# Two activation buffers of a two-block transformer kernel at other SBUF addresses

## What is computed

```python
gu = h @ w_gate_up            # 1024 x 5632
g, u = jnp.split(gu, 2, axis=-1)
return (jax.nn.silu(g) * u) @ w_down   # 2816 x 1024
```

## The kernel before

| Buffer | used by TensorE as | before | with the change |
|---|---|---|---|
| `whi`, `wlo` | weights, or moving in v2 and mdn | 0 | 0 |
| `xa` | moving; weights in v2 | 64 | 32 |
| `xb` | moving | 64 | 64 |
| `ghid` | moving | 64 | 0 |
| `hid` | weights | 0 | 0 |

## Time and profile before

### The profile page before, as it was taken

The page is one execution under the profiler, slowest core; times in us unless marked ns, Lnnn a source line. Parts: engine busy times, 40 slices in busy tenths (PEclk is TensorE's granted clock), DMA queues, the critical chain, the costliest instruction groups (busy, mean ns, idle before and its releaser), DMA issues.

```text
span 977.0 us, 19940 instructions
## 1 busy us (share of the span) xinstructions
PE 970.0 (99%) x7076; PEld 902.9 (92%) x7076; DVE 696.9 (71%) x1046; ACT 589.4 (60%) x1050; POOL 268.0 (27%) x241
## 2 busy tenths in 40 slices
PE   9999999999999999999999999999999999999998
PEld 7999899999998899999999888888889989998887
DVE  7987766665668778666565799987877877664443
ACT  7556755554557767545554678968585577664332
POOL 2431233220102223223210136542031546441000
PEclk9999999999999999999999999999999999999999
DMA  9785565655543245555455554654444536556531
GB/s 335 256 316 187 188 212 174 213 167 190 206 173 129 88 138 207 198 189 204 164 203 205 176 177 165 216 181 164 173 147 170 201 130 218 205 179 207 181 130 43
DMA packets 37712, 180.92 MB, mean 185 GB/s; under 512 B 3472, under 2 KB 7824, under 8 KB 19984
## 3 DMA queue, kind: packets, MB, share of 16 engines
q1 hardware_dynamic: 37504, 179.99, 52.5%
q10 hardware_dynamic: 144, 0.08, 0.1%
HBM read 179.01 MB, written 1.05 MB: 184 GB/s over the span
## 4 chain that ended last, share of the span: by engine, by line
PE 95%; DVE 2%; ACT 1%; issue 1%; POOL 1%; DMA 1%; SPq 0%; POOLq 0%; DVEq 0%
PE bank L502 26%; PE bank L496 19%; PE bank L498 17%; PE bank L500 17%; PE bank L540 4%; PE bank L539 4%; PE bank L538 4%; DVE wlo L1534 1%; DVE xa L1588 1%; PE bank L751 1%; PE bank L626 1%; DMA x<-in_x 1%; PE bank L735 1%; PE bank L765 0%; PE bank L976 0%
## 5 line engine op out<-in xcount | busy, mean ns | idle before, releaser
L1534 DVE TENSOR_TENSOR wlo<-raw,whi 128x1024 fp32r<-128x1024 f32 (+1 forms) x289 | 354.2, 1226 | 148.0 <-ACT whi L1009 147.1
L1009 ACT ACTIVATE whi<-raw 128x1024 fp32r<-128x1024 f32 (+2 forms) x289 | 302.1, 1046 | 202.2 <-PE bank L502 196.7
L502 PE MATMUL bank<-xa,wlo 128*128 128x256 f32 x1536 | 308.7, 277 | 0.0
L502 PEld LDWEIGHTS bank<-xa,wlo 128*128 128x128 f32 x1536 | 254.9, 188 | 22.9
L498 PE MATMUL bank<-xa,whi 128*128 128x256 f32 x904 | 227.3, 276 | 0.0
L500 PE MATMUL bank<-xa,whi 128*128 128x256 f32 x904 | 227.2, 276 | 0.0
L496 PE MATMUL bank<-xa,whi 128*128 128x512 f32 x632 | 203.3, 397 | 0.7 <-POOL wlo L2242 0.5
L498 PEld LDWEIGHTS bank<-xa,whi 128*128 128x128 f32 x904 | 169.7, 188 | 0.0
L500 PEld LDWEIGHTS bank<-xa,whi 128*128 128x128 f32 x904 | 169.7, 188 | 0.0
L2130 POOL TENSOR_TENSOR gate<-act,rbc 128x256 f32<-128x256 f32 x44 | 69.0, 1569 | 158.2 <-ACT act L1174 153.0
L496 PEld LDWEIGHTS bank<-xa,whi 128*128 128x128 f32 x632 | 99.6, 188 | 7.6 <-issue 1.7
(11 more groups left out here) (233 smaller groups left out, 1530.0 us busy)
## 6 DMA issues: line engine op xcount, KB each, us to landing
raw<-in_stream SPq DMA_DIRECT2D x137, 1024.0 KB, 4.8
raw<-in_stream SPq DMA_DIRECT2D x42, 512.0 KB, 4.8
raw<-in_stream SPq DMA_DIRECT2D x8, 768.0 KB, 4.1
bias<-in_bias SPq DMA_DIRECT2D x1, 3072.0 KB, 11.4
raw<-in_stream SPq DMA_DIRECT2D x8, 256.0 KB, 5.5
x<-in_x SPq DMA_DIRECT2D x4, 256.0 KB, 5.4
out<-x SPq DMA_DIRECT2D x3, 256.0 KB, 2.2
cons<-in_cons SPq DMA_DIRECT2D x1, 576.0 KB, 9.1
```

The source lines that it names most:

```text
L502: ins = pe.matmul(narrow, wlo[:, slot, at + i, :], X[:, k, 0, :], start=False, stop=last and i == len(tiles) - 1)
L1009: act.activation(whi[:, p, 0:kts, :].rearrange("p k m -> p (k m)"), src, ACT.Copy)\
L1534: dve.tensor_tensor(wlo[:, p, 0:kts, :].rearrange("p k m -> p (k m)"), src, whi[:, p, 0:kts, :].rearrange("p k m -> p (k m)").bitcast(F32) ...
```

## The change

The filler ahead of `xa` shrinks from 16 to 8 words of 4 bytes, and one of 8 words is put between `xa` and `xb`, so that `xb` and all behind it stay where they were. The filler ahead of `ghid` goes. No instruction, wait or transfer is added, taken away or moved: on all five engines the order of the instructions is the same.

```diff
         x = sb("x", [P, KT, TOK])
-        sb("before_xa", [P, 16])
+        sb("before_xa", [P, 8])
         xa = sb("xa", [P, KT, 2, TOK], F32R)
+        sb("before_xb", [P, 8])
         xb = sb("xb", [P, KT, 2, TOK], F32R)
...
         regiond = ExitStack()
-        regiond.enter_context(nc.sbuf_tensor("before_ghid", [P, 16], F32))
         ghid = regiond.enter_context(nc.sbuf_tensor("ghid", [P, FT, 2, TOK], F32R))
```

## The result

| | before | with the change |
|---|---|---|
| median, same chip | 985.19 us (981.31 to 987.43, 4 runs) | 1000.1 us (999.8 to 1000.33, 4 runs) |
| profiled execution, its own time | 978.75 us | 1000.33 us |
| its span | 977.0 us | 998.3 us |

The ratio of the medians is 1.0154, with a 95% interval of 1.0124 to 1.0184: slower by 1.5%, outside the range that was given. The two profiled executions differ by more, 21.3 us of span.

What follows compares the result with a forecast made beforehand. TensorE's matmul count times its start-to-start step was taken as the bound. Wide `xa` -3.3 and `xa` as weights -0.6, others 0, made -3.9 us, from 985.37 to 981.5 us; range 978.0 to 997.5.

Steps and rivals of the forecast that it cites:

- The clean step is a floor: Narrow matmuls of `xa` at 0.1133 us cannot step faster, so the change can only leave that step or break it.
- The forecast is wrong if the narrow step moves at all: Sign against the forecast: any change of the 0.1133 us narrow step; the wide one keeping its 5.52 us was the other.
- xa narrow: 2712 matmuls of 256 columns at L498, L500 and L502: taken as 0, bounds 0 to 11.3 or 18.1 us slower.
- a second influence: `xb` narrow, also 64 behind, stepped at 0.1175 us, 0.0042 more than `xa`; read as a clean and a slow rhythm.
- the lower of the two prices offered from above: Upper bound for narrow `xa` falling into the slow rhythm of `xb`: 2712 x 0.0042 = 11.3 us; the other was 18.1.
- The same step for ghid: 1056 narrow matmuls going to difference 0: taken as 0, from above 4.4 or 7.0 us slower.
- xa wide: 664 matmuls at L496 and L626 losing 0.005 us each: all taken as gone, -3.3 us; bounds -3.3 to +1.1.
- a matter of rhythm and half a step nearer to the clean case may suffice: Reason given for taking all 3.3 us of the wide `xa` loss as gone, and the 0.6 us as weights.
- xa as weights: 96 matmuls at L538 to L540 losing 0.0067 us each: taken as -0.6 us, bounds 0 and -0.6.
- `xb` and all behind it keep their places: nothing of their own: Term for the unmoved buffers, `xb`, `hid` and the attention's `bias`: no cost or gain counted.
- rivals 3 and 4: Narrow `xa` loses its clean rhythm, 11.3 us, chance 0.15; `ghid` alone does, 4.4 to 7.0 us, 0.10; both together 0.04.
- rival 5: Timed runs 6.6 us above the profile hold slow narrow matmuls, which the new placement avoids: 978.8 us, chance 0.06.

Runs made afterwards that it cites:

- the map: Kernels computing nothing of the reference, TensorE alone streaming at many operand distances; the second goes from wide to narrow pieces in 16-byte steps. Narrow loss 0.0 to 6.7 ns per step.
- the profile of 985.65 us: The unchanged kernel before, profiled again on the same chip: 985.65 us, with up0 clean and up1 and dn1 slow; a further execution took 979.78 us.
- the first map: TensorE alone, computing nothing of the reference, five streams per placement in 32-byte steps, a short matmul ahead of each; narrow loss 0.0 to 6.7 ns per step.

## Why the prediction was wrong

**What held.** The bound was read rightly: TensorE's pace is the time, no wait moved, and the whole difference lies in start-to-start steps. The clean step is a floor, as argued: no stretch of any run went under 0.1133. That addresses matter, and by the relation of the two operands, held too (everything 64 bytes later changed nothing). "The forecast is wrong if the narrow step moves at all" named the sign that came. The forecast was 981.5 us and the range ended at 997.5; measured were 1000.1.

**The step that failed, xa narrow.** "I take 0, because moving minus weights address is 64 in the clean rows 5 and 6 and 0 in the clean rows 7, and 32 lies between." Both halves fell. The dependence can't be interpolated: the map goes 0.0 at 112, 5.3 at 128, 0.0 at 192 and 5.9 at 208. And 64 is not a clean place but one with two rhythms; the earlier trace rows happened to show the clean one. The earlier trace rows had shown the slow one at the same distance, and I set it aside as a second influence instead of reading it as the price at hand. Measured 11.0 us, where the lower of the two prices offered from above was 11.3. That the two agree is in part luck: the price was that of `xb` at 64, and place 32 charges 4.45 ns in up0 and up1 but 3.33 elsewhere.

**The same step for ghid.** The 0 rested on the earlier trace rows, where each load of weights goes with 512 columns and the weights are the activation. With 256 columns, difference 0 costs 6.65 ns a step in every stream: 7.0 us, the upper bound. The prediction had the doubt ("though with twice the columns per weight load") and gave it 0.10.

**xa wide, the wrong sign.** Forecast -3.3, measured +2.6. The loss before was 4.5 us and not 3.3, since the one stretch of the earlier trace rows lies in a mild stage. The map has 3.3 or 6.6 ns per step at 32 and 2.5 at 64, so the sign is the place's, and the kernel's mean of 5.3 per step (7.0 us / 1328) lies between the map's two values. At 64 the kernel's mean is 3.4 against the map's 2.5, and what adds to it was not found. That the loss was "a matter of rhythm and half a step nearer to the clean case may suffice" was again interpolation.

**xa as weights.** Forecast -0.6, measured 0.0: 32 costs there what 64 does.

**Not in the sum.** `xb` narrow, unmoved, lost 1.9 us more: in o and bl it took the slow rhythm (0.00 to 4.44 ns a step), in which wo stood before. "`xb` and all behind it keep their places: nothing of their own" counted addresses and not what stands ahead of a stream.

**The rivals.** The profiled pair, +21.3 us, is rivals 3 and 4 together (11.3 + 7.0 = 18.3) with the wide and `xb` terms on top. Against the median only 15 us show, and rival 5's mechanism says why, with its sign turned: a gap of this size was slow narrow streams in the profile of 985.65 us, 6.2 of it up1 and dn1. I wrote that nothing in the trace ties the gap to this, and gave 0.06; that second profile ties it, while the timed runs themselves were not traced. By it the median execution of the kernel before had paid some 6 us already, so the change could only take 15 more. With the change all four runs lie within 0.53 us, although place 32 has two prices as well.

## What to carry to other kernels

Where TensorE is the bound, read its step from start to start, stretch by stretch, and compare like matmuls with each other; the busy share says 99% in both cases here. The distance between the starts of the moving operand and of the weights is worth mapping with TensorE alone, entered as the kernel enters it, before a buffer is moved: 192 bytes (of 256) behind the weights gave 978.4 to 979.7 us in 12 runs, 64 gave 978.5 to 990. A map shows which prices a place can charge and not which one the kernel will pay: 192 was slow in four of five streams of the first map and clean in nearly all of the kernel, and 32 paid more in the kernel than in any narrow stream of the maps. And when the runs of a kernel scatter in groups while one profile looks clean, profile it again: that profile may be the lucky execution, and a price read from one execution is then not the price of the kernel.

## What had not been expected of the hardware

- With a load of weights for each 256 columns in float32r, the step depends on the distance of two start addresses with a period of 256 bytes, not monotonically: 113.3 ns clean, 120.0 at distance 0, with neighbours 16 bytes apart that differ by up to 6.6 ns (96 and 112).
- One placement can have two steady rhythms (narrow, 0.0 or 4.4 ns at 64, 3.3 or 4.45 at 32), each kept over stages of 192 to 864 matmuls, and different in two executions of the same kernel. At 64 the slow one was kept from up0 to dn0 and from up1 to dn1. In the kernel before, the four groups that fit this span 9 us.
- Place 192 has the slow rhythm too, but `ghid` at 192 ran clean right behind slow streams of `xa` at 32, where `ghid` at 64 did not.

What produces the pattern stays open. It was seen that the relation of the addresses suffices, without any other engine; which reads meet there was not shown. Also open: what picks the rhythm on entry, and why the wide form at 64 costs more in the kernel than in the map. Not tried: 112 bytes, or 64 for bodies that are mostly wide with 192 for the narrow ones.
